# One decoder step on one core: the first expert gather taken from four of five token tiles, the last tile's rows added by products, two weight loads held until it has landed

## The chip, the cores and the metric

The kernel runs on one core of one Trainium2 chip. The metric is the device time of one execution in microseconds, lower is better. A core has PE (TensorE, matrix products), DVE (VectorE), ACT (ScalarE), POOL (GpSimd) and SP (SyncE, which here only issues transfers). They run their own instruction streams and meet through semaphores; 16 DMA engines move data for all of them.

## The reference

One layer of a hybrid decoder on 512 prompt tokens and 8 sample tokens, model width 1024, all in fp32. Two mixers in parallel (a causal pooling mixer and a Mamba-2 state-space mixer) feed one output projection with a residual. Then comes a mixture of experts: 32 experts in four groups, and each token goes to the best two of its best group. After it follow a gated per-layer input and a last norm.

```python
h = h + concat([pool_out, ssd_out]) @ w_out
u = rmsnorm(h, norm_ffn)
g_w, g_idx = top_k(softmax(u @ rg_w + rg_b), 1)          # one of 4 groups
e_w, e_idx = top_k(softmax(logits of that group), 2)     # two of 8 experts
h = h + sum over both: gate * (silu(u @ w_gate[e]) * (u @ w_up[e])) @ w_down[e]
h = h + sigmoid(rmsnorm(h, norm_ple) @ ple_gate_w + ple_gate_b) * (p @ ple_proj_w)
```

Every expert has a gate and an up matrix of 1024 x 256 and a down matrix of 256 x 1024, each 1 MB in fp32.

## The kernel before, in words

The 520 tokens lie in five tiles (`ROWS`: four of 128, one of 8 for the samples). After the mixers the output projection goes through them in `ORDER` = 0, 1, 4, 2, 3, two halves of 512 columns each; the last in that order is tile 3. For each half DVE adds the residual (`residual`, L1713). Then PE transposes the rows (`h_rows`), DVE takes them with the norm's gain (`take_h`, L1721), PE multiplies with the router's weights (`route`, L886), DVE makes logits (L1738), chooses two experts (`choose`), PE counts how many earlier tokens chose each expert (`count`, L896) and DVE turns this into a rank inside the expert (`rank`, ending in L1771). Beside this ACT sums the squares (L1256), POOL takes the inverse root (L1405, L1406), ACT scales the rows (L1271) and stores them to `u_rows` in DRAM (`store_row`, L1273).

The experts work on blocks of 64 tokens (`S`). Blocks 0 to 31 are the first 64 tokens of each expert; more tokens for an expert would fill extra blocks. Blocks 0 to 23 (`HEAD`) are written out, the others run in a loop of four. Two blocks are a pair and share one gather of 128 rows. The table of rows is made by `fill_slots` (L913): products of a one-hot matrix of ranks, weighted by token number, with the one-hot of experts, summed over all five tiles in a PSUM bank. A slot without a token reads as 4096 and is out of the gather's bounds, so it is skipped and stays zero in `G`. DVE turns the sums into integers (L1818, L1819). POOL waits for them and for all five stores of rows, then gathers pairs 0 and 1 by indirect transfers (L1483).

For a pair, PE transposes the gathered rows (`pair_rows`, L593; a transpose is one record in the trace, an fp32 product two), DVE takes them with the gain (`take_pair`, L1878). For a block, PE does `gate_up` (L989, L990), ACT the silu (L1288), DVE `gate_act` (L1882), PE transposes the activations (`act_rows`, L996; L1002 in the loop), DVE takes them (`take_act`, L1885), and PE does `down` (L1010) of a block after the next block's `gate_up`. ACT takes the result (L1293, L1294), POOL scatters a pair's rows (L1487). Before block 0 PE also fills the table of extra blocks (`fill_extra_slots`, L922), for which DVE has worked out ranks beyond 64 and offsets (L1836 to L1850), and in block 0 DVE counts the loop's rounds (`extra_blocks`).

The weights stay in seven slots for gate and up (`gu`) and five for down (`dn`), which are regions of one SBUF tensor that earlier stages have left. All loads are issued by SP in order: blocks 0, 1, 3 and 6 and four down matrices before and during the output products; gate and up of 2, 4 and 5 and the down matrix of 4 when the output products are over; from then on a down load when the block four before has its down product done (`s_Y_ready`, issued at L490) and a gate/up load when the block seven before has its gate/up done (`s_up_done`, L484 and L486).

## Time and profile before

| | us |
|---|---|
| median of 3 runs | 569.43 |
| lowest and highest | 569.17, 572.87 |
| the profiled execution | 570.61 |
| its span | 568.8 |
| PE busy in the span | 507.8 (89%) |
| DVE, ACT, POOL busy | 207.7, 154.1, 111.8 |
| moved by the queues | 144.72 MB, mean 254 GB/s |

The span runs from the first to the last instruction; the profiled execution's own time has 1.8 us around it. The page divides the span into 40 slices of 14.2 us. A row of a timeline gives the start, the time, engine, line, operation, what is written and read, and the number of records; in brackets stands how long the engine was idle before it and what released it. `L989` is line 989 of the kernel before.

### The profile page before, as it was taken

What the parts mean: (1) busy time and instruction counts of PE and PEld (TensorE: products, weight loads), DVE (VectorE), ACT (ScalarE), POOL (GpSimd) and SP (SyncE); (2) the same over time, 40 slices, a digit from 0 to 9 for tenths busy, and PEclk for the clock granted to TensorE, in tenths of its full rate; (3) what the DMA queues carried; (4) which work ended last, traced back from release to release, by engine and by line L of the source; (5) the groups of instructions that cost most, each with busy time, mean ns of one, the idle gap of its engine ahead of it and who ended that gap; (6) DMA issues with size and microseconds to landing.
All of it is one profiled execution on the core that took longest, in us unless ns stands there. A gap on an engine that the chain in (4) does not pass through costs nothing.

```text
span 568.8 us, 7815 instructions
## 1 busy us (share of the span) xinstructions
PE 507.8 (89%) x3098; PEld 312.2 (55%) x3098; DVE 207.7 (37%) x496; ACT 154.1 (27%) x315; POOL 111.8 (20%) x178
## 2 busy tenths in 40 slices
PE   5899999999999997199999999978776999999994
PEld 4688886768645554165555555544343554344443
DVE  1286496523033546432221121111110211169455
ACT  0435163103534121102222222211210223355223
POOL 1200048993001001101121111111011223022001
PEclk9999999999999999579999999999996999999999
DMA  8990000503449705949999999999999999640001
GB/s 290 418 295 3 1 1 10 213 1 68 170 163 400 328 9 199 414 142 341 418 417 415 416 417 416 414 416 417 416 413 382 413 413 365 217 196 39 3 37 74
DMA packets 40214, 144.72 MB, mean 254 GB/s; under 512 B 14522, under 2 KB 15162, under 8 KB 31076
## 3 DMA queue, kind: packets, MB, share of 16 engines
q1 hardware_dynamic: 33316, 132.79, 59.4%
q0 software_dynamic: 5152, 8.85, 4.2%
q10 hardware_dynamic: 1712, 2.62, 1.2%
q8 instruction: 23, 0.38, 0.3%
q14 instruction: 11, 0.09, 0.0%
HBM read 140.15 MB, written 14.19 MB: 271 GB/s over the span
## 4 chain that ended last, share of the span: by engine, by line
PE 44%; DMA 10%; DVE 3%; issue 2%; SPq 2%; ACT 1%; POOLq 0%; POOL 0%; DVEq 0%; ACTq 0%
PE PS L989 18%; PE PS L1092 10%; PE PS L1010 9%; DMA mem<-in_exp_w_down 5%; PE PS L593 4%; DVE mem L1878 2%; DMA u_rows<-mem 2%; DMA mem<-u_rows,idx_all 1%; DMA choice_rows<-mem,out_i 1%; DMA mem<-choice_rows 1%; SPq L484 1%; PE PS L834 1%; SPq L486 1%; PE PS L990 1%; PE PS L996 1%
## 5 line engine op out<-in xcount | busy, mean ns | idle before, releaser
L989 PE MATMUL PS<-mem 128*64 128x256 f32 x512 | 119.3, 387 | 6.8 <-DVE mem L1878 6.8
L990 PE MATMUL PS<-mem 128*64 128x256 f32 x512 | 119.3, 387 | 0.0
L989 PEld LDWEIGHTS PS<-mem 128*64 128x64 f32 x512 | 68.4, 139 | 43.2 <-DVE mem L1878 7.6
L1010 PE MATMUL PS<-mem 128*64 128x512 f32 x256 | 62.6, 610 | 18.1 <-issue 9.0
L633 PE MATMUL PS<-mem 128*128 128x260 f32 x320 | 73.3, 385 | 0.0
L990 PEld LDWEIGHTS PS<-mem 128*64 128x64 f32 x512 | 68.4, 139 | 0.0
L633 PEld LDWEIGHTS PS<-mem 128*128 128x128 f32 x320 | 59.8, 190 | 10.5 <-issue 1.5
L1882 DVE TENSOR_TENSOR mem<-PS,mem 64x256 f32<-64x256 f32 x32 | 13.7, 428 | 119.6 <-ACT mem L1288 119.6
L821 PE MATMUL PS<-mem 128*128 128x512 f32 x128 | 56.6, 595 | 0.0
L1092 PE MATMUL PS<-mem 128*128 128x512 f32 (+1 forms) x144 | 56.1, 547 | 0.0
L593 PEld LDWEIGHTS PS<-mem 128*128 128x128 f32 (+4 forms) x254 | 31.0, 170 | 45.5 <-issue 29.9
L593 PE MATMUL PS<-mem 128*128 128x128 f32 (+4 forms) x254 | 40.0, 289 | 13.5 <-DMA mem<-u_rows,idx_all 12.5
L1878 DVE TENSOR_TENSOR mem<-PS,mem 128x512 f32<-128x512 f32 x34 | 23.5, 692 | 75.3 <-PE PS L593 75.2
L1288 ACT ACTIVATE mem<-PS 64x256 f32<-64x256 f32 x32 | 12.0, 375 | 134.5 <-PE PS L990 134.5
L1010 PEld LDWEIGHTS PS<-mem 128*64 128x64 f32 x256 | 18.4, 139 | 43.6 <-issue 31.6
L1092 PEld LDWEIGHTS PS<-mem 128*128 128x128 f32 x144 | 27.0, 190 | 26.3 <-issue 25.5
L1405 POOL TENSOR_TENSOR mem<-mem 128x1 f32<-128x1 f32 (+1 forms) x20 | 4.5, 225 | 175.9 <-ACT mem L1256 85.2
L821 PEld LDWEIGHTS PS<-mem 128*128 128x128 f32 x128 | 23.8, 190 | 26.9 <-issue 26.8
L604 PE MATMUL PS<-mem 128*128 128x260 f32 x128 | 31.6, 412 | 6.8 <-DMA mem<-in_w_a 6.8
L1293 ACT ACTIVATE mem<-PS 64x512 f32<-64x512 f32 x32 | 18.9, 590 | 65.3 <-PE PS L1010 65.3
L604 PEld LDWEIGHTS PS<-mem 128*128 128x128 f32 x128 | 26.3, 207 | 11.3 <-DMA mem<-in_w_a 6.8
L1483 POOL DMA_INDIRECT mem<-u_rows,idx_all x15 | 15.3, 1021 | 79.4 <-PE PS L593 70.5
(270 smaller groups left out, 547.4 us busy)
## 6 DMA issues: line engine op xcount, KB each, us to landing
mem<-in_exp_w_down SPq DMA_DIRECT2D x32, 1024.0 KB, 21.2
mem<-in_exp_w_gate SPq DMA_DIRECT2D x32, 1024.0 KB, 18.9
mem<-in_exp_w_up SPq DMA_DIRECT2D x32, 1024.0 KB, 22.0
mem<-in_w_out SPq DMA_DIRECT2D x2, 2048.0 KB, 7.4
mem<-in_ple_gate_w SPq DMA_DIRECT2D x1, 4096.0 KB, 29.7
mem<-choice_rows SPq DMA_DIRECT2D x4, 1024.0 KB, 8.8
mem<-in_xT SPq DMA_DIRECT2D x4, 520.0 KB, 9.1
mem<-in_w_a SPq DMA_DIRECT2D x4, 512.0 KB, 9.9
```

What stands on the lines that cost most here:

```text
L593: return pe.transpose(dst, src, ident[0:n, 0:n])
L604: ins = pe.matmul(PS[A_BANKS[j][h]][:, 0:HALF], COLS[j][2][:, k, :], xg[k // 4][:, k % 4, h * HALF:(h + 1) * HALF], start=(k == 0), stop=( ...
L633: ins = pe.matmul(PS[b + h][:, 0:HALF], w[:, k, :], aT[:, k, h * HALF:(h + 1) * HALF], start=(k == 0), stop=(k == KT - 1))
L821: return pe.matmul(PS[OUT_BANKS[i][h]][:, :], mix_col(k, ORDER[i]), w_out[:, k, h * 512:(h + 1) * 512], start=(k == 0), stop=(k == KT - 1))
L989: pe.matmul(PS[0][0:S, 0:FF], rows_k, gu[slot][:, k, :], start=(k == 0), stop=(k == KT - 1))
L990: ins = pe.matmul(PS[1][S:2 * S, 0:FF], rows_k, gu[slot][:, KT + k, :], start=(k == 0), stop=(k == KT - 1))
L1010: ins = pe.matmul(PS[4 + h][h * S:(h + 1) * S, :], actT[:, s % 2, f * S:(f + 1) * S], dn[slot][:, f, h * 512:(h + 1) * 512], start=(f == 0 ...
L1092: ins = pe.matmul(PS[4 if q else 2 * (i % 2) + h][:, 0:w], uTr[:, i % 2, k * P:(k + 1) * P], w_ple[:, k, h * 512 + q * w:h * 512 + (q + 1) ...
L1293: A(ysb[rows, s // 2, 0:512], PS[4][0:S, :], ACT.Copy)
L1483: pool.indirect_dma_start(G[:, q, :], None, u_dram, bass.IndirectOffsetOnAxis(ap=idx, axis=0), bounds_check=TOK - 1, oob_is_err=False).the ...
L1878: tt(uT[:, slot, half * 512:half * 512 + 512].rearrange("p (k c) -> p k c", c=P), tiles(PS[6 + half][:, :]), g_ffn[:, 4 * half:4 * half + ...
L1882: tt(act_tok[:, s % 2, :], PS[1][S:2 * S, 0:FF], sg[:, s % 2, :], ALU.mult).then_inc(s_act_ready, 1)
```

## The change

- The first pair's slots are filled from the first four tiles only (`first_pair_slots`, two columns of experts, bank 1), right after the last output product. DVE turns them into indices ahead of `take_h(4, 1)`. POOL gathers pair 0 by them, once the four stores of rows are there. `G`'s first half is set to zero long before, its second half after the first pair is through.
- Rows of tile 3 that belong to the pair are added by products: DVE makes a selection matrix (`first_pair_rows`: which of the 128 slots each token of the tile has, times its inverse root), and PE sums, in banks 0 and 2, the transposed gathered rows (a product with the identity) and the tile's rows times the selection. These two banks are first cleared by a product (`first_pair_zero`), and DVE takes the sum (`take_rows_of`).
- The table of all tiles goes to bank 3 and is ready after the first pair; pair 1 is gathered by it. Its transposes and `fill_extra_slots` move into block 1, DVE's work on extra ranks (`extra_choices`) into block 0 and `extra_blocks` into block 1.
- SP waits for the landing of the first gather (`g_full[0]`) before it issues gate and up of blocks 4 and 5.
- The down slot of block 4 changes places in SBUF with part of a gate/up slot and is loaded with that of block 2, during the output products.
- Tile 3's part of `u_rows` is first filled with prompt rows by a copy inside DRAM, and ACT's store of that tile waits for the copy.

```diff
-        gu = [at(r, 2 * KT, FF) for r in (R_gu + GU, R_gu + 2 * GU, R_gu + 3 * GU, R_gu, R_xc, R_xc + GU, R_aT)]
-        dn = [at(r, 2, D) for r in (R_dn, R_dn + DN, R_samp + 1024, R_d3, R_aT + GU)]
+        gu = [at(r, 2 * KT, FF) for r in (R_gu + GU, R_gu + 2 * GU, R_gu + 3 * GU, R_gu, R_xc, R_xc + GU, R_aT + DN)]
+        dn = [at(r, 2, D) for r in (R_dn, R_dn + DN, R_samp + 1024, R_d3, R_aT)]
...
+            tl = ORDER[NT - 1]
+            sp.dma_start(u_dram[tl * P:(tl + 1) * P, :], a["x_prompt"][0, tl * P:(tl + 1) * P, :]).then_inc(st_shift, 16)
...
             load_down(dn_slot(2), bass.ds(2, 1))
+            load_down(dn_slot(4), bass.ds(4, 1))
 
             sp.wait_ge(s_outp_done, 2 * NT)
             load_gate_up(gu_slot(2), bass.ds(2, 1))
+
+            sp.wait_ge(g_full[0], 16)
             for b in (4, 5):
                 load_gate_up(gu_slot(b), bass.ds(b, 1))
-            load_down(dn_slot(4), bass.ds(4, 1))
...
+            def first_pair_zero():
+
+                pe.wait_ge(s_outp_out, 9)
+                for half in range(2):
+                    pe.matmul(SEL[half][:, :], bef[:, 0:1].to_broadcast((P, P)), const[:, 0:256].bitcast(BF16),
+                              start=True, stop=False)
+
+            def first_pair(rows, place, half, last_part):
+
+                for q in range(4):
+                    ins = pe.matmul(SEL[half][:, q * P:(q + 1) * P], rows.rearrange("s (p k) -> s k p", k=KT)[:, 4 * half + q, :],
+                                    place, start=False, stop=last_part and q == 3)
+                if last_part:
+                    ins.then_inc(s_T_done, 1)
+
+            def first_pair_slots():
+
+                pe.wait_ge(s_pos_ready, NT - 1)
+                for i in range(NT - 1):
+                    for k in range(2):
+                        t = ORDER[i]
+                        choice = oh[:, t, k * NE:(k + 1) * NE].rearrange("p (b q) -> p q b", q=2)
+                        for q in range(2):
+                            ins = pe.matmul(PS[1][q * S:(q + 1) * S, 0:2], posh[:, 2 * t + k, :], choice[:, q, 0:2],
+                                            start=(i == 0 and k == 0), stop=(i == NT - 2 and k == 1))
                 ins.then_inc(s_tab_done, 1)
...
             out_half(4, 1, 6, KT)
+            first_pair_slots()
             h_rows(4, 1)
             route(4)
+            first_pair_zero()
             for i in range(NT - 1):
                 fill_slots(i)
             count(4)
+            pe.wait_ge(g_full[0], 16)
+            for half in range(2):
+                first_pair(G[:, 0, :], ident, half, False)
+            pe.wait_ge(s_sel_ready, 1)
+            for half in range(2):
+                first_pair(h1[:, ORDER[NT - 1], :], sel, half, True)
             fill_slots(4)
             count_all()
...
-            pe.wait_ge(g_full[0], 16)
-            pe.wait_ge(s_lg_out, NT)
-            pair_rows(0, 0)
-            pe.wait_ge(s_cnt_taken, 1)
-            pair_rows(0, 1)
-            fill_extra_slots()
...
-                if b % 2 == 0:
-                    pe.wait_ge(g_full[(b // 2 + 1) % 2], 16 * ((b // 2 + 1) // 2 + 1))
-                pair_rows((b // 2 + 1) % 2, b % 2)
+                if b == 1:
+                    pe.wait_ge(g_full[1], 16)
+                    pe.wait_ge(s_lg_out, NT)
+                    pe.wait_ge(s_cnt_taken, 1)
+                    pair_rows(1, 0)
+                    pair_rows(1, 1)
+                    fill_extra_slots()
+                elif b >= 2:
...
-            for p in range(2):
-                gather(p, idx_all[:, p:p + 1])
+            pool.wait_ge(s_tab_ready, 1)
+            pool.wait_ge(u_stored[0], 32)
+            pool.wait_ge(u_stored[1], 32)
+            pool.wait_ge(st_shift, 48)
+            gather(0, idx_i[0][:, 0:1])
+            pool.wait_ge(s_T_done, 2)
+            step(pool.memset(G[:, 1, :], 0.0))
+            pool.wait_ge(s_tab_ready, 2)
+            pool.wait_ge(u_stored[0], 48)
+            gather(1, idx_all[:, 1:2])
...
+            def first_pair_rows(i):
+
+                t = ORDER[i]
+                R = ROWS[t]
+                step(tt(hit[0:R], iota_s[0:R, :].unsqueeze(1).to_broadcast((R, 2, S)),
+                        rk[0:R, t, :].unsqueeze(2).to_broadcast((R, 2, S)), ALU.is_equal))
+                for k in range(2):
+                    ins = stt(selk[0:R, k], hit[0:R, k].unsqueeze(1).to_broadcast((R, 2, S)), rstd[0:R, 5 + t:6 + t],
+                              oh[0:R, t, k * NE:k * NE + 2].unsqueeze(2).to_broadcast((R, 2, S)), ALU.mult, ALU.mult)
+                step(ins)
+                tt(sel[0:R, :].rearrange("p (q s) -> p q s", s=S), selk[0:R, 0], selk[0:R, 1], ALU.add).then_inc(s_sel_ready, 1)
```

How it moves instructions, in three places. PE between the last count of tile 3 and block 0; the names in brackets are the semaphores waited for. Before:

```order
L896 MATMUL PS<-mem 128x32 [waits s_pos_ready,s_oh_ready]
L896 MATMUL PS<-mem 128x32 x4
L913 MATMUL PS<-mem 64x16 [waits s_pos_ready]
L913 MATMUL PS<-mem 64x16 x3
L902 MATMUL PS<-mem 128x32 x5
L593 MATMUL PS<-mem 128x128 [waits s_lg_out,g_full0]
L593 MATMUL PS<-mem 128x128 x3
L593 MATMUL PS<-mem 128x128 [waits s_cnt_taken]
L593 MATMUL PS<-mem 128x128 x3
L922 MATMUL PS<-mem 64x12 [waits s_slot_ready]
L922 MATMUL PS<-mem 64x12 x19
L989 MATMUL PS<-mem 64x256 [waits w_full4,s_uT_ready]
```

The same place after the change:

```order
L905 MATMUL PS<-mem 128x32 [waits s_pos_ready,s_oh_ready]
L905 MATMUL PS<-mem 128x32 x4
L948 MATMUL PS<-mem 128x128 [waits g_full0]
L948 MATMUL PS<-mem 128x128 x7
L948 MATMUL PS<-mem 128x128 [waits s_sel_ready]
L948 MATMUL PS<-mem 128x128 x7
L922 MATMUL PS<-mem 64x16 [waits s_pos_ready]
L922 MATMUL PS<-mem 64x16 x3
L911 MATMUL PS<-mem 128x32 x5
L1035 MATMUL PS<-mem 64x256 [waits w_full4,s_uT_ready]
```

The wait for the gather stands ahead of the last tile's slots, 16 products (L948) are in the place of the eight transposes, and the extra slots are gone from here.

SP around the end of the output products, before:

```order
L490 DMA mem<-in_exp_w_down 128x2x1024 [waits st_hs]
L484 DMA mem<-in_exp_w_gate 128x2048 [waits s_outp_done]
L486 DMA mem<-in_exp_w_up 128x2048
L484 DMA mem<-in_exp_w_gate 128x2048
L486 DMA mem<-in_exp_w_up 128x2048
L484 DMA mem<-in_exp_w_gate 128x2048
L486 DMA mem<-in_exp_w_up 128x2048
L490 DMA mem<-in_exp_w_down 128x2x1024
L484 DMA mem<-in_exp_w_gate 128x2048 [waits s_up_done]
L486 DMA mem<-in_exp_w_up 128x2048
```

After:

```order
L495 DMA mem<-in_exp_w_down 128x2x1024 [waits st_hs]
L495 DMA mem<-in_exp_w_down 128x2x1024
L489 DMA mem<-in_exp_w_gate 128x2048 [waits s_outp_done]
L491 DMA mem<-in_exp_w_up 128x2048
L489 DMA mem<-in_exp_w_gate 128x2048 [waits g_full0]
L491 DMA mem<-in_exp_w_up 128x2048
L489 DMA mem<-in_exp_w_gate 128x2048
L491 DMA mem<-in_exp_w_up 128x2048
L489 DMA mem<-in_exp_w_gate 128x2048 [waits s_up_done]
L491 DMA mem<-in_exp_w_up 128x2048
```

One down load has moved ahead of the wait for the output products, and four loads stand behind the new wait.

DVE from the last residual to the last logits, before:

```order
L1713 TENSOR_TENSOR mem<-PS,mem 128x512 [waits s_outp_done]
L1721 TENSOR_TENSOR mem<-PS,mem 128x512 [waits s_uTr_done,s_lg_done]
L1738 SCALAR_TENSOR_TENSOR mem<-PS,mem 128x40 [waits s_lg_done,s_inverse_root]
L1744 MAX mem<-mem 128x8 [waits s_lg_out]
L1745 MAX_INDEX mem<-mem 128x8 [waits own_dve]
```

After:

```order
L1770 TENSOR_TENSOR mem<-PS,mem 128x512 [waits s_outp_done]
L1882 TENSOR_SCALAR out_i<-PS 128x1 [waits s_tab_done]
L1883 TENSOR_SCALAR idx_i<-out_i 128x1 [waits own_dve]
L1778 TENSOR_TENSOR mem<-PS,mem 128x512 [waits s_uTr_done,s_lg_done]
L1795 SCALAR_TENSOR_TENSOR mem<-PS,mem 128x40 [waits s_lg_done,s_inverse_root]
L1801 MAX mem<-mem 128x8 [waits s_lg_out]
```

The two steps for the first pair's indices stand ahead of the take of the last rows.

## Rows read from the trace of the kernel before

**Rows 1.** The page: rate of the queues in 40 slices, and the last chain's shares

```profile
GB/s 290 418 295 3 1 1 10 213 1 68 170 163 400 328 9 199 414 142 341 418 417 415 416 417 416 414 416 417 416 413 382 413 413 365 217 196 39 3 37 74
...
PE 44%; DMA 10%; DVE 3%; issue 2%; SPq 2%; ACT 1%; POOLq 0%; POOL 0%; DVEq 0%; ACTq 0%
PE PS L989 18%; PE PS L1092 10%; PE PS L1010 9%; DMA mem<-in_exp_w_down 5%; PE PS L593 4%; DVE mem L1878 2%; DMA u_rows<-mem 2%; DMA mem<-u_rows,idx_all 1%; DMA choice_rows<-mem,out_i 1%; DMA mem<-choice_rows 1%; SPq L484 1%; PE PS L834 1%;
```

**Rows 2.** Windows: length, busy PE, PEld, DVE, ACT, POOL; granted clock, DMA share, GB/s

```profile
220.00:225.00 5.00, 3.60 (x52) 3.34 (x52) 2.66 (x12) 1.87 (x3) 2.49 (x3) 1.00 0.90 321
225.00:230.00 5.00, 1.18 (x18) 0.93 (x18) 3.42 (x20) 0.98 (x3) 0.00 (x0) 0.50 0.99 366
...
240.00:245.00 5.00, 4.07 (x50) 3.74 (x50) 1.38 (x2) 0.00 (x0) 0.99 (x1) 0.50 0.39 152
245.00:250.00 5.00, 5.00 (x34) 2.93 (x34) 0.00 (x0) 0.00 (x0) 0.00 (x0) 0.61 0.25 66
...
255.00:260.00 5.00, 4.48 (x34) 2.26 (x32) 1.88 (x7) 1.56 (x3) 0.99 (x1) 1.00 0.78 274
...
420.00:430.00 10.00, 4.04 (x36) 2.50 (x35) 1.20 (x3) 0.82 (x2) 1.54 (x4) 0.82 1.01 408
```

**Rows 3.** The chain that ended last: start, time, what

```profile
223.22 8.89 DMA u_rows<-mem
...
233.14 7.75 DMA mem<-u_rows,idx_all
240.93 1.97 PE PS L593 x8
...
245.15 0.51 PE PS L989
...
251.04 0.44 DVE mem L1882
...
255.47 1.72 PE PS L1010 x8
...
403.67 27.83 DMA mem<-in_exp_w_down
```

**Rows 4.** Timeline of SP, which issues the loads

```profile
219.61 0.33 SPq L484 DMA_DIRECT2D mem<-in_exp_w_gate  x1
...
222.63 0.45 SPq L490 DMA_DIRECT2D mem<-in_exp_w_down  x1
250.63 0.33 SPq L484 DMA_DIRECT2D mem<-in_exp_w_gate  x1
...
257.22 0.38 SPq L490 DMA_DIRECT2D mem<-in_exp_w_down  x1
...
270.27 0.38 SPq L490 DMA_DIRECT2D mem<-in_exp_w_down  x1
```

**Rows 5.** Timeline of PE, DVE and POOL around the first gather

```profile
177.60 1.04 PE L593 MATMUL PS<-mem 128*128 128x128 f32 x8
...
219.62 0.69 DVE L1713 TENSOR_TENSOR mem<-PS,mem 128x512 f32<-128x512 f32 x1 [0.76 <-PE PS L821]
...
221.41 0.55 POOL L1406 TENSOR_TENSOR mem<-mem 128x1 f32<-128x1 f32 x1
...
222.89 1.11 PE L913 MATMUL PS<-mem 128*64 128x16 f32 x32
...
227.01 0.54 DVE L1771 TENSOR_SCALAR mem<-mem 128x64 f32<-128x64 f32 x2
...
231.47 0.17 DVE L1836 CAST int_w<-mem 128x10 int32<-128x10 f32 x1
...
232.34 0.19 POOL L1480 TENSOR_TENSOR mem<-mem 128x1 f32<-128x1 f32 x1 [8.63 <-DMA u_rows<-mem]
...
235.30 0.16 DVE L1857 TENSOR_TENSOR mem<-mem 128x5 f32<-128x5 f32 x1
```

**Rows 6.** All gathers (L1483)

```profile
DMA to landing us min/median/max: 4.2/8.0/8.8
```

More of the change, by code:

```diff
@@ L1877, in take_pair @@
             def take_pair(slot, half):
[L1878 to L1879 removed]
+                take_rows_of(PS[6 + half], slot, half)
             def gate_act(s):
```

98 lines of the change are left out of this document (60 added, 38 removed).

## The prediction

> **What bounds the kernel now.** I read the page first. Its row of GB/s stands at 413 to 418 from the 20th of the 40 slices up to the 33rd, with one dip to 382, and its chain gives the two expert products (L989, L1010) 27% of the span and waits for transfers 10% [rows 1]: a long stretch in which expert weights stream in, with PE behind them. The windows say which of the two is the limit: from 420 to 430 us PE works 4.0 of 10 us and the queues still move 408 GB/s [rows 2]. The chain shows the last place where this decides. A down load issued at 403.67 lands 27.83 us later, PE starts only then (431.5), and the chain goes through PE's blocks again, with no wait for a transfer until the experts' end [rows 3]. One block asks for three loads of 1.05 MB, 7.5 us at 417 GB/s, and PE needs 6.5 us for it (13.05 us between the down loads issued at 257.22 and 270.27, two blocks [rows 4]). So the end hangs on when that down load lands, and this on when the stream of loads begins to flow without gaps. That beginning is the stretch before block 0. In the windows the queues are full up to about 242, then run at 152 and 66 GB/s, and even from 255 to 260 at 274 [rows 2]: all seven gate/up slots hold weights, and nothing can be loaded before block 0 frees one. SP's rows say the same: no issue between 222.63 and 250.63 [rows 4]. What holds block 0 is the chain from 223 on: the last tile's row store 8.89 us, the gather 7.75, transposes, extra slots, block 0 at 245.15 [rows 3]. Both transfers stand among seven weight loads (7.3 MB) issued from 219.61 to 222.63.
>
> **The first gather, forward by some 13 us.** The slots of the first pair now come from four tiles. The 16 added products are of the kind of L913, whose 16 for four tiles stand as 32 records (two each) and took 1.11 us [rows 5]. They end near 220.7, in a time in which PE waited for the residual of 219.62 anyway. Two small DVE steps (0.17 us each, as row 231.47 [rows 5], and a little between them) give the indices at 221.2, and delay take_h(4,1) and all choices behind it by 0.3 us. POOL has the last inverse root done at 221.96 and needs about 0.9 us to the issue (232.34 to 233.14 in before [rows 3, 5]): issue at 222.9. The landing is the main unknown. From below it is the 4.2 us of the fastest gather [rows 6]: 227.1. From above it is the 7.75 us of row 233.14: 230.7. I take 228: only one block's gate and up (2.1 MB), the gather and the last store (0.5 MB each) are left on the queues, 3.1 MB or 7.5 us of flow from about 221.2, which puts the end of all of them at 228.7. (The window 220 to 225 moved 321 of 417 GB/s, so the flow began 1.2 us into it, 1.5 us after the issue.)
>
> The Trainium skill (DMA: Bandwidth & Descriptors, section Queues, rings and completion order) has each DMA engine go round the queue rows packet by packet, so that a small transfer takes its share beside a large one. By that, the store and gather in before would have shared the flow and been through in a fraction of their times; the rows of 8.89 and 7.75 us [rows 3] speak for much more queueing. By the rule alone the gather would land nearer to 227, and holding the loads would buy little; by the rows the hold is what shortens it. The sum goes by the rows.
>
> **The last tile by products.** For the tokens of the last tile a selection matrix is needed: rank(4) ended at 227.55 [rows 5], now 227.85, then four DVE steps on 128x128 (0.3 us each, between the 0.17 us of row 231.47 and the 0.69 of the 128x512 step of row 219.62 [rows 5]): ready at 229.0. In place of 8 transposes of one record each PE has 8 products with G and 8 with the tile's rows, of two records each: two groups of 16 records. Eight transposes of 128 columns took 1.04 us at the full clock (row 177.60 [rows 5]) and 1.97 at half (row 240.93 [rows 3]), so each group of 16 costs 2.1 to 3.9 us. The windows show the clock at 1.00 up to 225 and at 0.50 from 225 to 245, with PE busy 1.2 of 5 us in the first of these [rows 2]. The added records (1.1 us of slots, two 512-column products to clear the banks) do not change that picture much, so I take mostly half clock, 3.5 us each: G part 228 to 231.5, tile part to 235.0, the second take by DVE 0.75 us (a 128x512 step has 0.69) to 235.75. Block 0 then begins at 235.8; bounds 231.7 (landing 227.1, full clock, the selection matrix last) and 239.3 (230.7, half clock). Before it began at 245.15: 9.4 us earlier.
>
> **Block 0 and 1.** gate_up(0) took 245.15 to 250.63, 5.5 us, its first part at half clock (the window to 250 has 0.61 on average, later ones 1.00 [rows 2]). At full clock it is 3.7: from 250.63 to the down product of 255.47 are 4.84 us, of which silu and gate_act take 0.85 (to 251.48) and the transposes of the activations some 0.3 [rows 3]. Now PE has worked through from 228, so the clock should be back earlier in the block: I take 4.4, bounds 3.7 and 5.5. It ends at 240.2. Behind its gate_act DVE now runs the steps that were at 231.47 to 235.46, 4.0 us [rows 5], before it takes block 0's activations. Silu and gate_act need 0.85 us before, the take some 0.3 after: ready 5.2 us after the end of gate_up(0), 0.35 later than PE's own 4.84. With down(0), 1.72 [rows 3], it is 6.9 us in all, where before it was 6.6 (250.63 to 257.22 [rows 4]). The first down slot comes free at 247.1, before 257.22: **10.1 us earlier**. The second gather is issued when the indices of all tiles are there, at about 236.3, and even with 7.75 us lands at 244.1, 3 us ahead of need; its transposes and the extra slots (before ahead of block 0) now lie in block 1 and delay block 2 by some 1.3 us, which costs nothing as long as the transfers are the limit.
>
> **The stream.** The held loads (two blocks' gate/up, 4.2 MB) flow from 228.3 + 1.5 = 229.8, with two gathers of 0.5 MB 12.6 us, to 242.4. The next gate/up is issued at 240.2 and adds 5.0 us, to 247.4; the first down and the next gate/up are issued at 247.1 and flow from 248.6. So the gap is 1.2 us, as it was before (250.63 + 1.5 + 5.0 = 257.1, flow again at 258.7). The cost of holding is idle flow from about 228 to 230, and it is covered, because block 0 is the later of the two. From here both kernels issue the same loads in the same order, and the queue is behind: one block's loads alone need 7.5 us, and its halves of a gather and a scatter come on top, against 6.5 us on PE. So the landing that PE waits for at 431.5 comes 10.1 us earlier, and everything behind it keeps its length. The fifth down load moves to about 170, where 1 MB is 2.5 us at the end of the loads before the output products; none of these is waited for until block 0. Because of it 4.2 MB and not 5.2 are held, which the sum above has in it; in before the megabyte went into time that ended idle. The copy of the last tile's prompt rows (0.5 MB) runs near 40 us, 1.3 us of queues in a stretch where the page has the queues almost empty (3 GB/s in the fourth slice [rows 1]). Both I put at 0, bounds 0 and 1.3.
>
> Sum: profiled execution 570.61 (span 568.8 and 1.8 around it) less 10.1 is 560.5. The median of the runs is 569.43, 1.2 below the profiled one; I predict the median, **559.3 us**.
>
> **The rivals.**
> A. *The clock stays up and the gather lands at its floor.* Block 0 from 231.7, gate_up 3.7, down slot at 242.3. Then the loads limit: 227.4 + 1.5 + 12.6 + 5.0 = 246.5 against 258.7: 12.2 us, 557.2. For it: PE gets more work in 220 to 225 than before. Against: the clock fell although PE had worked 3.6 of the 5 us before, and PE still waits some 2 us for the gather.
> B. *The gather is as slow as ever.* 7.75 us, half clock throughout: block 0 at 239.3, its end at 244.3, slot at 251.2: 6.0 us, 563.4. For it: all gathers of the trace have a median of 8.0 us [rows 6]. Against: most of them ran in a full stream, which is what is held here.
> C. *Transfers hide it.* Block 0 comes early, but the held 4.2 MB (10 us), which were covered by the wait for the gather, now stand in the stream in full, so that the down load of 403.67 is not earlier. This needs the flow to restart late. The same mechanism decides the other side: with a landing at g the stream is back at its old place when g + 1.8 + 12.6 + 5.0 + 1.2 = 258.7, so at g = 238.1 nothing is gained, and behind that point every us of landing is lost. At 244.5 the kernel would be **slower** by 6.4 us, 575.8. For it: a transfer of 0.5 MB did take 8.89 us. Against: 15 us from the issue at 222.9 to the point of no gain, 21 to this price, with less than half of the old bytes on the queues.
> D. *The change doesn't do what it says*: the first gather waits for something else on POOL or SP's hold is released late, say at 235: 3 us left, 566.3.
>
> **How the numbers follow.** Forecast 0.50, A 0.20, B 0.18, D 0.06, C 0.06 (half of it slower by over 1%, half within). One per cent, 5.7 us, is about what a measurement of this kernel can tell from no change. Faster by over 1% holds the forecast, A and B except its slow edge (0.04): 0.86; within 1% that edge, D and a half of C: 0.11; slower 0.03. The range goes from 555.8 (A with 1.3 us to spare) to 564.6 (beyond B by 1.2); beyond it lie D and C and little of A.
>
> **What would show it.** Right: the first gather issued near 223 and landing near 228; PE's products behind it; block 0 at 234 to 237; SP's next gate/up issue near 240 and down issue near 247; GB/s at 414 or so from about 248; the wait for a down load ending near 421.4; from it to the end the same length. Wrong: a landing after 231, a granted clock of 0.5 past 240, SP waiting on the gather with empty queues for over 3 us, or a new wait in block 1 for the second gather or for DVE's moved steps; or the down wait near 431 in spite of an early block 0, which would be C.

## The result, and the profile after

| | us |
|---|---|
| kernel before, median of 4 runs beside it | 570.12 (569.17 to 572.87) |
| kernel after, median of 4 | 564.64 (561.8 to 566.05) |
| ratio | 0.9888, 95% interval 0.9854 to 0.9922 |
| profiled execution after | 561.8, span 559.9 |

The change makes the kernel 1.1% faster by the ratio: 5.5 us by these medians, 4.4 to 8.3 by the interval. The forecast was 10.1 us less, 559.3, with a range of 555.8 to 564.6: the median of 564.64 lies on its upper edge. The same kernel measured again beside eleven runs of before gave 563.88 against 571.31, ratio 0.9864 [0.9835, 0.9893].

The stages that the prediction used can be read off SP and the chain. T1 is SP's issue of block 2's loads (the end of the output products), D the first down issue behind block 0, W the end of the wait for the late down load. In before: 219.61, 257.22 [rows 4], 431.50 (403.67 + 27.83 [rows 3]), span end 568.8. After, SP's timeline (start, duration, queue, line, operation, what is written and read):

```profile
217.91 0.34 SPq L489 DMA_DIRECT2D mem<-in_exp_w_gate  x1
...
228.91 0.33 SPq L489 DMA_DIRECT2D mem<-in_exp_w_gate  x1
...
241.35 0.33 SPq L489 DMA_DIRECT2D mem<-in_exp_w_gate  x1
...
248.59 0.38 SPq L495 DMA_DIRECT2D mem<-in_exp_w_down  x1
```

and the chain that ended last, against [rows 3]:

```profile
220.65 8.24 DMA mem<-u_rows,idx_i
228.94 7.93 PE PS L948 x32
236.89 0.70 DVE mem L1893
237.63 0.43 PE PS L1035
...
241.35 0.39 ACT mem L1338
...
246.61 1.94 PE PS L1056 x8
...
396.34 26.34 DMA mem<-in_exp_w_down
```

The store of the last tile and the extra slots are gone from the chain, as intended; a gather of 8.24 us and 7.93 us of products stand there instead. W is 396.34 + 26.34 = 422.68. Stage by stage:

| us | T1 | T1 to D | D to W | W to end of span |
|---|---|---|---|---|
| before | 219.61 | 37.61 | 174.28 | 137.3 |
| after | 217.91 | 30.68 | 174.09 | 137.2 |
| forecast for after | 219.6 | 27.5 | 174.3 | 137.3 |

So the change's own gain in this pair of profiles is 6.9 us from T1 to D. The other 1.7 us of the profiled 8.8 lie before T1, where the only edits are two transfers in a quiet stretch, and they have nothing to do with the change. The granted clock (third number from the end of each line) goes with them; first before, then after, from 25 to 50 us:

```profile
25.00:50.00 25.00, 23.70 (x178) 20.31 (x178) 17.39 (x38) 10.74 (x19) 1.27 (x3) 0.93 0.68 230
```

```profile
25.00:50.00 25.00, 23.70 (x186) 20.49 (x185) 18.87 (x43) 11.82 (x19) 1.22 (x3) 1.00 0.75 251
```

All fourteen profiles of this study follow this: those with 1.00 in that window have T1 between 217.9 and 218.1 (of the kernel with block 2's loads held too, T1 is worked out from POOL's rows), those with 0.93 between 219.5 and 220.3, the one with 0.86 at 221.1. Eight of the fourteen have a lower clock there, among them the second profile of the changed kernel, whose first has 1.00. The size fits: 0.07 of 25 us is 3.5 us at half clock, in which a busy PE loses 1.7. The runs of before alone lie between 568.7 and 574.8 us. Stages measured from T1 are therefore compared below beside the medians.

The page's rates and the windows that answer to [rows 1, 2] (length, busy PE, PEld, DVE, ACT, POOL, clock, DMA share, GB/s):

```profile
GB/s 291 413 316 39 1 1 13 214 1 61 180 140 394 422 24 165 303 314 418 415 414 416 416 415 416 416 416 418 416 409 381 411 412 347 244 147 39 2 37 75
```

```profile
220.00:225.00 5.00, 3.13 (x49) 2.44 (x49) 2.93 (x17) 1.15 (x1) 1.60 (x3) 0.83 1.03 356
225.00:230.00 5.00, 1.06 (x4) 1.07 (x5) 2.30 (x10) 1.71 (x3) 0.00 (x0) 0.50 0.55 184
230.00:235.00 5.00, 5.00 (x23) 5.00 (x22) 0.03 (x1) 0.00 (x0) 0.00 (x0) 0.65 0.87 367
235.00:240.00 5.00, 4.78 (x43) 3.80 (x44) 3.46 (x13) 0.00 (x0) 1.96 (x2) 1.00 1.02 431
240.00:245.00 5.00, 3.99 (x38) 2.41 (x34) 3.22 (x12) 0.38 (x1) 0.99 (x1) 1.00 0.85 285
```

The hole of 152 and 66 GB/s that before has from 240 to 250 is gone; the page reaches 414 or more in its 19th slice. The clock is back at 1.00 by 235, in before by 250.

### The profile page after: what moved, and what is told of

It reads as the page before. It is cut to its first block, busy times and chain, and to the rows that moved or that the text cites. A ratio compares the mean times of both kernels' runs of the same rounds, so it can differ in the third digit from the quotient of the medians.

```text
span 559.9 us, 7942 instructions
## 1 busy us (share of the span) xinstructions
PE 512.1 (91%) x3155; PEld 317.1 (57%) x3156; DVE 209.0 (37%) x502; ACT 154.1 (28%) x315; POOL 111.8 (20%) x179
## 4 chain that ended last, share of the span: by engine, by line
PE 48%; DMA 6%; DVE 3%; issue 1%; SPq 1%; ACT 0%; POOLq 0%; POOL 0%; DVEq 0%; ACTq 0%
PE PS L1035 18%; PE PS L1140 10%; PE PS L1056 10%; DMA mem<-in_exp_w_down 5%; PE PS L602 4%; PE PS L973 3%; DVE mem L1893 2%; DMA mem<-u_rows,idx_i 1%; PE PS L948 1%; PE PS L843 1%; PE PS L1036 1%; PE PS L1042 1%; PE PS L1048 0%; SPq L489 0%; PE PS L931 0%
## 5 line engine op out<-in xcount | busy, mean ns | idle before, releaser
L1035 PE MATMUL PS<-mem 128*64 128x256 f32 x512 | 117.3, 382 | 6.5 <-DVE mem L1893 6.5
L1036 PE MATMUL PS<-mem 128*64 128x256 f32 x512 | 117.4, 382 | 0.0
L1035 PEld LDWEIGHTS PS<-mem 128*64 128x64 f32 x512 | 67.5, 137 | 41.8 <-DVE mem L1893 7.2
L1056 PE MATMUL PS<-mem 128*64 128x512 f32 x256 | 64.2, 624 | 15.9 <-DMA mem<-in_exp_w_down 8.6
L1036 PEld LDWEIGHTS PS<-mem 128*64 128x64 f32 x512 | 67.5, 137 | 0.0
L602 PEld LDWEIGHTS PS<-mem 128*128 128x128 f32 (+4 forms) x246 | 29.3, 168 | 31.3 <-issue 30.5
L1056 PEld LDWEIGHTS PS<-mem 128*64 128x64 f32 x256 | 18.6, 142 | 41.9 <-issue 29.1
L1140 PEld LDWEIGHTS PS<-mem 128*128 128x128 f32 x144 | 27.0, 190 | 26.7 <-issue 25.9
L830 PEld LDWEIGHTS PS<-mem 128*128 128x128 f32 x128 | 23.8, 190 | 26.9 <-issue 26.8
L602 PE MATMUL PS<-mem 128*128 128x128 f32 (+4 forms) x246 | 37.6, 284 | 0.0
L613 PEld LDWEIGHTS PS<-mem 128*128 128x128 f32 x128 | 25.8, 203 | 11.1 <-DMA mem<-in_w_a 6.8
L1532 POOL DMA_INDIRECT mem<-u_rows,idx_all x14 | 14.1, 1010 | 68.5 <-PE PS L602 67.3
## 6 DMA issues: line engine op xcount, KB each, us to landing
mem<-in_exp_w_up SPq DMA_DIRECT2D x32, 1024.0 KB, 21.1
```

The source lines that it names most:

```text
L602: return pe.transpose(dst, src, ident[0:n, 0:n])
L613: ins = pe.matmul(PS[A_BANKS[j][h]][:, 0:HALF], COLS[j][2][:, k, :], xg[k // 4][:, k % 4, h * HALF:(h + 1) * HALF], start=(k == 0), stop=( ...
L830: return pe.matmul(PS[OUT_BANKS[i][h]][:, :], mix_col(k, ORDER[i]), w_out[:, k, h * 512:(h + 1) * 512], start=(k == 0), stop=(k == KT - 1))
L1035: pe.matmul(PS[0][0:S, 0:FF], rows_k, gu[slot][:, k, :], start=(k == 0), stop=(k == KT - 1))
L1036: ins = pe.matmul(PS[1][S:2 * S, 0:FF], rows_k, gu[slot][:, KT + k, :], start=(k == 0), stop=(k == KT - 1))
L1056: ins = pe.matmul(PS[4 + h][h * S:(h + 1) * S, :], actT[:, s % 2, f * S:(f + 1) * S], dn[slot][:, f, h * 512:(h + 1) * 512], start=(f == 0 ...
```

## The experiments

Twelve kernels, each timed in rounds beside the kernel before. "Land" is the first gather's landing, counted from T1 like D. D to W is the column in which the stream of loads would take something back. It comes from one profile each, and the two profiles of the changed kernel differ in it by 3.5 us (174.1 and 177.6), so that a difference of 1 to 3 us there proves nothing by itself.

| run | median, runs | ratio to before, 95% | land | T1 to D | D to W |
|---|---|---|---|---|---|
| before (profile) | 570.12 to 571.31 | | 21.3 | 37.6 | 174.3 |
| after (first profile) | 564.64 (4) | 0.9888 [0.9854, 0.9922] | 11.0 | 30.7 | 174.1 |
| e1 after again | 563.88 (7) | 0.9864 [0.9835, 0.9893] | 11.9 | 31.6 | 177.6 |
| e2 no hold | 564.12 (6) | 0.9881 [0.9848, 0.9913] | 13.2 | 32.9 | 173.8 |
| e3 tile's part first | 561.82 (6) | 0.9819 [0.9787, 0.9851] | 11.2 | 29.3 | 175.5 |
| e4 neighbouring columns | 561.57 (4) | 0.9815 [0.9777, 0.9853] | 10.9 | 29.0 | 174.3 |
| e5 block 2 held too | 562.93 (4) | 0.9853 [0.9819, 0.9886] | 8.2 | 28.0 | 176.6 |
| e6 store later | 561.51 (4) | 0.9826 [0.9792, 0.9860] | 8.8 | 28.5 | 174.2 |
| e7 fifth down late | 563.82 (6) | 0.9854 [0.9824, 0.9884] | 11.0 | 30.8 | 175.0 |
| e8 before with SP's part alone | 564.30 (6) | 0.9874 [0.9847, 0.9900] | 15.7 | 31.8 | 175.1 |
| e9 permuted rows, tile first | 560.36 (6) | 0.9808 [0.9772, 0.9844] | 9.3 | 26.9 | 176.4 |
| e10 permuted rows, store later | 560.10 (6) | 0.9800 [0.9771, 0.9830] | 8.6 | 26.7 | 175.4 |
| e11 before, down load early | 571.69 (12) | 1.0016 [0.9994, 1.0038] | 21.1 | 37.5 | 174.6 |
| e12 as e9, no hold | 560.17 (6) | 0.9830 [0.9800, 0.9860] | 12.8 | 27.9 | 174.7 |

(e1 to e4, e5 to e8, and e9 to e11 shared their runs of before; medians of before 571.31, 570.92, 571.11, and 570.85 for e12. In e12 the landing is a reading between PE's rows, to some 0.3 us.)

**e1, the changed kernel again.** No edit.

> The changed kernel once more, as the control of this group and to see how far its executions lie apart: from 561.8 to 566.05 so far. Theory 1 (the gain is the earlier block 0 alone): relative to the end of the output products (SP's issue of block 2's loads at 217.91), the wait for the late down load ends 204.8 us after it and is 211.9 in before, so the ratio should be 0.987 to 0.988. Theory 2 (the profiled execution's 1.7 us before the output products' end belong to the change too): 0.984. If a second profile has the same clock windows as the first, the spread is not in the place where block 0 starts.

The median is 563.88; its profiled execution is the slowest of seven (567.82) and has D to W at 177.6 instead of 174.1. The down load that PE waits for late is issued 151.2 us behind D (402.40 in this chain) instead of 147.8 (396.34). Why the same loads took 3 us more in between was not found; from 10 to 15 us behind D the queues moved 374 GB/s and not 419, which is 0.5 us of it. The gather took 9.15 us here and 8.24 in the first profile. T1 to D, 31.6, is within 1 us of the first profile.

**e2, the hold taken away.**

```diff
-            sp.wait_ge(g_full[0], 16)
             for b in (4, 5):
                 load_gate_up(gu_slot(b), bass.ds(b, 1))
```

> The changed kernel without SP's wait for the first gather: loads of blocks 4 and 5 are issued at once. Theory 1 (what is on the queues when the gather is issued delays it): 4.2 MB more stand among gather and store, the gather takes 11 to 15 us from its issue instead of 8.2, block 0 starts 3 to 6 us later, and the end is 3 to 6 us later than the control's. Theory 2 (the queues share, and a gather takes some 8 us whatever is on them): the gather lands within 1 us of the control's, the loads of 4 and 5 are through by 235, block 0 starts as before and the end is the same or up to 1 us earlier.

The chain's row for the gather:

```profile
220.84 10.40 DMA mem<-u_rows,idx_i
```

1.3 to 2.2 us more than in the two profiles with the hold, with 4.2 MB of loads added beside it, 10 us of flow at 417 GB/s. That is less than theory 1 had and more than theory 2. So most of the held bytes would not have stood ahead of the gather. The median does not move by a measurable amount.

**e3, the tile's part of the products first.** PE waits for the selection matrix, does the products with the tile's rows, and only then waits for the gather.

```diff
-            pe.wait_ge(g_full[0], 16)
-            for half in range(2):
-                first_pair(G[:, 0, :], ident, half, False)
             pe.wait_ge(s_sel_ready, 1)
             for half in range(2):
-                first_pair(h1[:, ORDER[NT - 1], :], sel, half, True)
+                first_pair(h1[:, ORDER[NT - 1], :], sel, half, False)
+            pe.wait_ge(g_full[0], 16)
+            for half in range(2):
+                first_pair(G[:, 0, :], ident, half, True)
```

> The changed kernel with the two groups of products in the other order: the last tile's rows times the selection first (the selection matrix is ready 1.7 us before the gather lands), the gathered rows when they have landed. Theory 1 (PE's products behind the gather hold block 0, and block 0 holds the stream): block 0 starts 1.7 to 2.0 us earlier relative to the end of the output products, SP issues the next gate and up as much earlier, and the end is 1.5 to 2 us earlier than the control's. Theory 2 (the held loads are the limit, block 0 is covered): block 0 is earlier, the end moves by less than 0.5 us.

PE starts the 32 records at 229.39, 1.5 us ahead of the landing at 230.93, and needs the same 7.91 us. D comes 1.3 to 2.3 us earlier, the median is 2.1 us less than e1's. Half of the products had been waiting for a transfer that they don't read.

**e4, stationary operands of neighbouring columns.** A product reads 128 columns side by side instead of every eighth; the first pair's features then stand in another order than the weights', so that its results are not the layer's, with the same instructions and bytes.

```diff
-rows.rearrange("s (p k) -> s k p", k=KT)[:, 4 * half + q, :],
+rows[:, (4 * half + q) * P:(4 * half + q + 1) * P],
```

> The changed kernel with the stationary operand of the 16 products taken from 128 neighbouring columns instead of every eighth; the features of the first pair are then in another order than the weights' (that part of the computation is changed), while all counts and sizes stay. Theory 1 (a weight load from every eighth column costs 336 ns and this, not the clock, sets 0.247 us a record): weight loads fall to some 230 ns at half clock and 190 at full, the 32 records take 5.5 to 6.5 us instead of 7.9, and block 0 starts 1.4 to 2.4 us earlier. Theory 2 (the clock sets it): weight loads stay at 336 ns and the 32 records at 7.9 us.

The line's weight loads (ns min/median/max, first and last start), in the changed kernel and here:

```profile
L948 PEld LDWEIGHTS PS<-mem x32: 312/336/339, 228.9 to 236.3; 128*128 128x128 f32 x32
```

```profile
L948 PEld LDWEIGHTS PS<-mem x32: 192/333/338, 231.2 to 237.2; 128*128 128x128 f32 x32
```

Windows of 1 us of that line alone show it by clock (busy PE with records, busy PEld with records, clock, share, GB/s), in the changed kernel

```profile
232.00:233.00 1.00, 1.00 (x6) 1.00 (x6) 0.50 0.97 410
...
235.00:236.00 1.00, 1.00 (x6) 1.00 (x5) 1.00 1.07 451
```

and in e9, which has the same operands as e4:

```profile
230.00:231.00 1.00, 1.00 (x6) 1.00 (x6) 0.50 1.02 434
231.00:232.00 1.00, 1.00 (x9) 1.00 (x9) 0.82 0.98 410
232.00:233.00 1.00, 1.00 (x11) 0.94 (x9) 1.00 1.02 434
```

A record that crosses the border of a window is counted in both. The single records of the trace start 0.24 us apart with every eighth column, at either clock; with neighbouring columns they start 0.21 us apart at 1.2 GHz and 0.11 at 2.4 GHz. Only the stationary operand differs, so at the full clock the weight load sets the pace, and not the product; reading across columns costs there about what the low clock would cost. At the low clock it costs little. The 32 records of e4 take 6.40 us instead of 7.93, and the median is 2.3 us less than e1's.

**e5, block 2's loads held too.** The wait for the gather stands ahead of all three blocks' loads.

```diff
             sp.wait_ge(s_outp_done, 2 * NT)
-            load_gate_up(gu_slot(2), bass.ds(2, 1))
-
             sp.wait_ge(g_full[0], 16)
+            load_gate_up(gu_slot(2), bass.ds(2, 1))
```

> The changed kernel with block 2's gate and up held behind the first gather too, so that nothing of the weights is on the queues when it is issued. Theory 1 (what is on the queues delays the gather: 8.2 us with 2.1 MB, 10.4 with 6.3 MB in the run without the hold, so some 0.5 us per MB): the gather lands 6.5 to 7.2 us after its issue, 1 to 1.5 us earlier. Theory 2 (in an empty queue it takes the 4.2 us of the fastest gather of the trace): 4 us earlier. For the time: 6.3 MB and two gathers, 17.6 us, then flow from its landing, so the stream is at its old place at landing + 1.8 + 17.6 + 5.0, some 3 to 5 us later than in the changed kernel by theory 1: slower by 1 to 4 us, since block 0 no longer covers it.

The gather takes 5.50 us, between the two theories, and D comes at 28.0, 2.7 us earlier than in after, yet the median is only 0.9 us less than that of e7, timed in the same rounds (the expectation had it slower by 1 to 4). The flow that was not used while the queues stood empty is missing later: from T1 to D the queues moved 298 GB/s, 8.3 MB, and in after 316 GB/s, 9.7 MB, a difference of 3.3 us of flow. D to W is 2.5 us longer (176.6). Its windows show the empty stretch (140 and 189 GB/s) and then a stream without a gap:

```profile
220.00:225.00 5.00, 3.16 (x50) 2.47 (x49) 2.93 (x17) 1.15 (x1) 1.64 (x3) 0.84 0.44 140
225.00:230.00 5.00, 3.77 (x16) 3.77 (x16) 2.34 (x10) 1.71 (x3) 0.00 (x0) 0.50 0.56 189
230.00:235.00 5.00, 4.78 (x33) 4.53 (x34) 1.48 (x4) 0.00 (x0) 0.79 (x1) 0.98 1.01 426
235.00:240.00 5.00, 3.99 (x36) 2.46 (x38) 3.16 (x14) 0.38 (x1) 2.17 (x3) 1.00 1.02 424
```

**e6, the last store behind the gather.**

```diff
                 if i == NT - 1:
                     act.wait_ge(st_shift, 48)
+                    act.wait_ge(g_full[0], 16)
```

> The changed kernel with ACT's store of the last tile's rows (0.5 MB) held until the first gather has landed. Theory 1 (the store, issued 0.9 us behind the gather, shares the engines with it and slows it): the gather takes 6 to 7 us instead of 8.2 and block 0 starts 1 to 2 us earlier, the end 1 to 2 us earlier. Theory 2 (the gather is slow for another reason): 8 us as before, the second gather waits a little, the end within 0.5 us of the control.

The gather, with block 2's 2.1 MB beside it but no store:

```profile
222.54 6.03 DMA mem<-u_rows,idx_i
```

D at 28.5, D to W unchanged, and a median 2.3 us less than that of e7, timed in the same rounds, from one line.

**e7, the fifth down load back behind the held ones.** The `load_down` of slot 4 stands again behind the loads of blocks 4 and 5.

> The changed kernel with the fifth down load back at its old place in SP's order, behind the held loads. Theory 1 (the stream has gaps of 2 to 3 us in all between block 0 and the first down load, which take up the megabyte): within 0.7 us of the control. Theory 2 (from the landing of the gather on the stream is the limit, and every megabyte counts): 2.5 us slower.

Nothing changes: 563.82 against 563.88, T1 to D 30.8.

**e8, the kernel before with SP's part alone.** The fifth down slot moved and loaded early, the loads of blocks 4 and 5 held until the gather has landed; the gather of all five tiles, the transposes and the extra slots as in before.

```diff
             load_down(dn_slot(2), bass.ds(2, 1))
+            load_down(dn_slot(4), bass.ds(4, 1))

             sp.wait_ge(s_outp_done, 2 * NT)
             load_gate_up(gu_slot(2), bass.ds(2, 1))
+            sp.wait_ge(g_full[0], 16)
             for b in (4, 5):
                 load_gate_up(gu_slot(b), bass.ds(b, 1))
-            load_down(dn_slot(4), bass.ds(4, 1))
```

> The kernel before with only SP's part of the change: the fifth down load early, the loads of blocks 4 and 5 held until the first gather has landed. Gather and store stay where they were. Theory 1 (the early gather and the products carry the gain, and lighter queues give a gather 1 to 2 us, a store 2 to 3): the last store lands 5 to 6 us after its issue instead of 8.9, the gather then takes 6.5 to 7.5, block 0 starts 3 to 5 us earlier relative to the end of the output products; the held loads flow from some 235 on, 12.6 us, so the stream is 1 to 3 us ahead of before at the first down load. The end is 1 to 3 us earlier than before, not 7. Theory 2 (the hold does nothing, as between the control and the run without it): block 0 as in before, but now the loads follow the gather: 1 to 3 us slower than before.

564.30 us, 0.4 us from the whole change. The chain, to be read against 8.89 and 7.75 in [rows 3]:

```profile
223.31 6.80 DMA u_rows<-mem
...
231.13 4.29 DMA mem<-u_rows,idx_all
235.47 1.97 PE PS L595 x8
237.44 2.25 PE PS L924 x40
239.69 0.51 PE PS L991
```

The store is 2.1 us shorter, the gather 3.5, and D comes 5.8 us earlier. Neither theory had this: theory 1 gave SP's part 1 to 3 us, and it is worth 6.6.

**e9 and e10, the weight loads mended for good.** ACT writes each scaled row with the features in the order in which the products read them, so that every stationary operand of them, and of all later pairs' transposes, is 128 neighbouring columns. The last tile's part is taken from this scaled row (the inverse root is then left out of the selection matrix). e9 has the tile's part first, e10 the store behind the gather.

```diff
-                A(row[0:R, i % 2, :], h1[0:R, t, :], ACT.Copy, scale=rstd[0:R, 5 + t:6 + t])
+                A(row[0:R, i % 2, :].rearrange("r (k p) -> r k p", k=KT),
+                  h1[0:R, t, :].rearrange("r (p k) -> r k p", k=KT), ACT.Copy, scale=rstd[0:R, 5 + t:6 + t])
...
-G[:, slot, :].rearrange("s (p k) -> s k p", k=KT)[:, k, :]
+G[:, slot, k * P:(k + 1) * P]
```

> The changed kernel, with the features of every scaled row written by ACT in the order in which the products read them, so that all stationary operands of the 16 products are 128 neighbouring columns (the same for the transposes of later pairs), the last tile's part taken from the scaled row and put ahead of the gather's part. Theory (the time before block 0 is 16 weight loads of 336 ns in pairs behind the later of gather and selection): contiguous loads take about 190 ns, each group of 16 records some 2.9 us instead of 3.95; the tile part starts when the selection matrix is ready, 9.3 us after SP issued block 2's loads, ends at 12.3, the gather has landed at 11, the gather's part ends at 15.3 against 18.9: first down load 27.1 us after block 2's, 3.6 earlier than in the changed kernel (30.7), median about 560.5. Rival (the loads are the limit once block 0 is this early): the first down load is earlier, but the stretch from it to the end of the wait for the late down load grows from 174 to 176 or more and the median stays at 561.5 to 562. Rival (ACT's scaling into a spread layout is slower than 1.16 us): the last store starts later by the difference and the table of all rows with it; nothing else moves.

> As the run before, but the gather's part stays ahead of the tile's, and the store of the last tile's rows waits until the first gather has landed. Theory (the gather shares the queues with two loads and a store; without the store it took 6.0 us instead of 8.2): the gather lands 8.8 us after SP issued block 2's loads, both groups of products end at 14.8, first down load 26.6 us after block 2's (30.7 in the changed kernel), median about 560. Rival (the loads are the limit): the stretch from the first down load to the end of the wait for the late one grows by what was gained, median 561.5, as with the store held back alone.

T1 to D fell to 26.9 and 26.7, as expected. The medians, 560.36 and 560.10, are 10.7 and 11.0 us below before's 571.11 and come where the theories had them (560.5 and 560), not at the rivals' 561.5. D to W is 176.4 and 175.4, inside what the two profiles of the changed kernel span, so it does not show that the loads took a part back. e9's order had no part in it: its products started at 227.43, when the selection matrix was ready, and by then the gather had landed (SP's held issue is at 227.27). In e9 ACT's scaling took 2.16 us instead of 1.15:

```profile
220.41 2.16 ACT L1320 ACTIVATE mem<-mem 128x1024 f32<-128x1024 f32 x1 [0.98 <-ACT mem L1305]
```

which put the store 1 us later. The gather took 6.5 us instead of 8.2; that the later store is the reason is likely by e6, but was not tested.

**e11, the kernel before with the down load early and nothing held.** e8 without its wait.

> The kernel before with only the fifth down slot moved and loaded during the output products; its loads of blocks 4 and 5 are not held, the gather, the store and the transposes are as before. Theory (in the run with the kernel before and SP's part alone, the hold took 2.1 us from the store of 8.89 us and 3.5 us from the gather of 7.75, and this was its gain of 6 us): here 6.3 MB still lie before and among the store and the gather, so the store takes about 8.5, the gather 7, block 0 begins 0.5 to 1.5 us earlier, and the median is within 1.5 us of the kernel before, 569.5 to 571. Rival (the megabyte of the fifth down load, which stood between the store and the gather, made most of the wait): store 7, gather 5, median 565 to 566.

571.69 us, no change; store 8.86, gather 7.58. So the gain of e8 is the hold's.

**e12, e9 without the hold.**

> The kernel with permuted rows and the tile's part of the products first, but with the loads of blocks 4 and 5 not held. Theory (once block 0 starts this early the loads are the limit, and the hold costs as much flow as it saves in the gather): the gather takes 9.5 to 10.4 us instead of 6.5 and lands some 13 us after SP issued block 2's loads; the tile's part is through by then, the gather's part ends at 16, the first down load is issued at 28 (26.9 with the hold), the stretch behind it is back at 174 (176.4 with the hold), median 559 to 561, the same as with the hold (560.4) within 1 us. Rival (the hold still carries the gain): the first down load at 29 or later and the stretch behind it no shorter than 176, median 563 or more.

560.17 us, equal to e9. The gather lands 3.5 us later and D comes 1.0 later. D to W is 1.7 shorter, as if the hold cost in flow what it saves in the gather, but one profile each does not show this.

## Why the prediction was right in direction and some 5 us too far

From T1 to D the forecast had a gain of 10.1 us and the two profiles of the changed kernel show 6.9 and 6.0; most of the rest of the 5 us is the base (below). The way was right, and the number only just inside its range.

**What bounds the kernel, and the stages behind D: right.** In the first profile D to W and W to the end kept their lengths (174.1 and 137.2 against 174.3 and 137.3), so the whole gain is in when the first down slot comes free. (In e1 D to W was 3.3 us longer than in before.) The late down load decides as before.

**T1 to D, term by term.** Forecast 27.5, measured 30.7 in the first profile:

| step of the prediction | forecast | measured | difference |
|---|---|---|---|
| T1 to the landing | 8.4 (228 less 219.6) | 11.0 | +2.6 |
| landing to block 0: two groups of 3.5, take | 7.8 | 8.7 | +0.9 |
| gate_up(0) | 4.4 | 3.7 | -0.7 |
| its end to the first down slot | 6.9 | 7.2 | +0.3 |

The step that failed is the landing, "the main unknown", with bounds of 4.2 to 7.75 us for the gather and 5.1 taken. The issue came 2.7 us behind T1, 0.6 earlier than forecast, and the gather took 8.24, beyond the upper bound. The sum behind the choice let 3.1 MB flow at 417 GB/s until 228.7, 9.1 us behind T1. The flow did end close to that, at some 9.5, though less was moved (260 GB/s over the 10.98 us to the landing, 2.85 MB): the queues were at full share at a lower rate, and the share falls only after 227. The landing came 1.2 us after the gather's last row:

```profile
222.00:224.00 2.00, 0.90 (x32) 0.81 (x28) 1.69 (x11) 0.00 (x0) 0.00 (x0) 0.82 1.02 360
224.00:226.00 2.00, 0.32 (x5) 0.21 (x5) 1.45 (x8) 0.00 (x0) 0.00 (x0) 0.50 0.96 272
...
227.00:228.00 1.00, 0.00 (x0) 0.00 (x0) 0.44 (x3) 0.45 (x3) 0.00 (x0) 0.50 0.36 139
228.00:229.00 1.00, 0.07 (x1) 0.07 (x1) 0.00 (x0) 1.00 (x1) 0.00 (x0) 0.50 0.02 8
```

So in these rows a gather and a store to DRAM keep the engines as busy as weights do while moving fewer bytes. The gather is also smaller than the sum had it. The DMA view of 220.6 to 229 us (packets, MB, share of the engines) has for POOL's queue

```profile
q0 software_dynamic: 144, 0.21, 7.0%
```

which are 52 rows of 4 KB and small packets: the slots without a token move no row. So size is not what makes it long. It starts late: its first row moves 4.5 us after the issue in after, at 225.2, 4.7 in e2 and 1.9 in e5, where no weights are on the queues. The same view of 217.9 to 225.1 us lists no packet of q0, and on SP's queue 2.01 of block 2's 2.1 MB. Why it starts when it does is not shown.

What each neighbour costs the gather is what the runs give: 5.50 us with the store alone (e5), 6.03 with block 2's loads alone (e6), 8.1 to 9.15 with both (after, e1, e3, e4, e7), 10.40 with 4.2 MB more (e2). The gather of all five tiles takes 4.29 on queues that stood empty at its issue (e8).

**The hold.** The prediction took the hold to be what shortens the gather, by the rows of 8.89 and 7.75, and cited the Trainium skill (DMA: Bandwidth & Descriptors, section Queues, rings and completion order) for the contrary: engines go round the queues packet by packet, so holding should buy little. In before both transfers did suffer, and the hold alone gives them 5.6 us back (e8 against before, e11 for the control). In the changed kernel it saves 1.3 to 2.2 us in the gather and nothing that the median shows (e2). The rule is nearer to e2: 4.2 MB more, 10 us of flow, cost at most 2.2 us, and the first row moved as early as with the hold. Why the store and the gather of before suffer so much more was not found.

**Two cures for one wait.** With the medians, before 571, e8 564.3 (the hold alone), e2 564.1 (the early gather, the products and the early down load, which by e11 is worth nothing), both 563.9. Each takes away the store's and the gather's time among the loads; once one is in, the other has 0.2 to 2.2 us of T1 to D left (31.8 and 32.9 against 30.7 and 31.6) and no more than 0.4 us of the median. The early gather takes the store off the path, but puts 7.9 us of products behind the landing, where 1.97 of transposes and 2.25 of extra slots stood. The prediction never priced the parts of the change one without the other.

**The products: too cheap by 0.45 us per group, and sized from the wrong rows.** They were put at 3.5 us per group, mostly at the low clock, and took 3.95. The clock was low for 4.6 of the 7.9 us. In the other 3.3 the full clock gave nothing back, because of the operand: the weight loads take 336 ns at both clocks (e4). The term had its ends (2.1 and 3.9) scaled from transposes. The lower came from the row of 177.60, whose operand is neighbouring columns, as its loads show:

```profile
L593 PEld LDWEIGHTS PS<-mem x8: 140/140/143, 177.2 to 178.3; 128*128 128x128 f32 x8
```

The transposes of gathered rows read every eighth column, and even they say little of products: at the full clock their load takes 193 ns, and 140 with neighbouring columns (the second pair's transposes, first in after, then in e9), while the products' goes from 192 to 336:

```profile
L602 PEld LDWEIGHTS PS<-mem x8: 186/193/208, 248.5 to 249.3; 128*128 128x128 f32 x8
```

```profile
L602 PEld LDWEIGHTS PS<-mem x8: 137/140/143, 244.8 to 245.5; 128*128 128x128 f32 x8
```

The Trainium skill (SBUF — State Buffer, section Door 1: The DMA port swizzle) states that fp32 reads that go to a new 16-byte line each time pay for it; every eighth fp32 column is 32 bytes on. The trace agrees at the full clock (336 ns against 192) and shows hardly any difference at the low one (336 against 333).

**gate_up(0) and DVE.** With PE at work through 229 to 237 the clock was back before block 0, and 3.7 us, the lower bound, was right. The end of block 0 to the down slot took 7.24: PE waited 0.36 us for the take behind DVE's moved steps, as forecast, and the down product took 1.94, not 1.72.

**What was put at nothing.** The moved down load is indeed worth nothing measurable (e7, e11). The copy of prompt rows has no run of its own; T1 is the same with it and without it at the same clock from 25 to 50 us (217.91 in after and 217.90 in e11, 219.53 in e1 and 219.61 in before). Block 2's delay does not show in the first profile's D to W.

**The base.** The forecast subtracted from 569.43, the median of three runs. The median of before in later batches is 570.85 to 571.31, some 1.5 us higher. The stretch near 30 us is worth 1.7 us between profiles and may be the reason; for runs without a profile this is not shown.

**Rivals.** B is the case that came true in its landing and its time: it had the landing 11.1 us behind T1 (230.7), D at 31.6 and 563.4 us; measured were 11.0 to 11.9, 30.7 to 31.6 and 563.9 to 564.6. It had a chance of 0.18, the forecast 0.50. What spoke against it, that most gathers ran in a full stream, was worth less than the row of all gathers with its median of 8.0 us [rows 6]. A's early clock came with it. C appears in part where more flow is left idle (e5). D did not occur. The chances were also added up wrongly: forecast, A and B less its slow edge are 0.84 and not 0.86, and within 1% are 0.13 and not 0.11.

## What to carry to other kernels

When a wait has two causes, price each edit alone as well as both: two edits that remove one wait are worth little more than one, and the simpler (e8: one wait on the issuing queue, with a slot moved) may do. Before turning transposes into products, look at the step between the columns of the stationary operand, and read the load's own row. A transfer that others wait for is to be kept clear of stores that nobody waits for; moving one store behind it was worth as much here as reordering the products.

The best versions measured, 560.1 to 560.4 us, need the permuted rows. There a microsecond on the path to block 0 seems to give less than itself: from e3 to e9 D comes 2.4 us earlier and the median falls by 1.5, and e12 has its D 1.0 later than e9 and the same median. That the weight stream has become the limit again is the likely reason, and not shown.

## What the runs showed of the hardware that was not expected

- The fp32 weight load of 128 columns for a product: 192 ns with neighbouring columns at the full clock and 333 at half; 336 at both when it takes every eighth column. ACT's copy of 128x1024 with one side spread took 2.16 us instead of 1.15.
- The first pair's gather moved 52 rows of 4 KB and took 5.5 to 10.4 us by what was beside it; its first row moved 1.9 us after the issue without weights on the queues and 4.5 us with block 2's loads and the store. The queues moved as little as 272 GB/s at a share of 0.96 with a gather and a store in them, against 415 with weights alone.
- Profiles of one kernel differ by 1.6 us at T1, one with a granted clock of 1.00 from 25 to 50 us and one with 0.93, long before the place of the change. A difference between two profiles is to be taken stage by stage.
